# The second FFN product of a two-layer DiT step by seven block products for eight

## What the kernel must compute

```python
x = x + g1 * o
h = modulate(rmsnorm(x, p['norm_ffn_g']), sh2, sc2)
gt, up = jnp.split(h @ p['ffn_w_in'], 2, axis=-1)
return x + g2 * ((jax.nn.silu(gt) * up) @ p['ffn_w_out'])
```

## Time and profile before

| what | value |
|---|---|
| three runs | 1826.86, 1824.64, 1828.18 us |
| median | 1826.86 us |
| profiled execution, span | 1825.5 us (the page gives no other time for it) |
| granted TensorE clock, mean | 0.996 of full speed |
| PE busy | 1741.5 us, 95% |
| DVE, ACT, POOL busy | 58%, 44%, 20% |

### The profile page before, as it was taken

The page is one execution under the profiler, slowest core; times in us unless marked ns, Lnnn a source line. Parts: engine busy times, 40 slices in busy tenths (PEclk is TensorE's granted clock), DMA queues, the critical chain, the costliest instruction groups (busy, mean ns, idle before and its releaser), DMA issues. The chain is left out here.

```text
span 1825.5 us, 46192 instructions
## 1 busy us (share of the span) xinstructions
PE 1741.5 (95%) x19693; PEld 1629.2 (89%) x19693; DVE 1064.4 (58%) x2330; ACT 803.0 (44%) x1729; POOL 370.7 (20%) x306
## 2 busy tenths in 40 slices
PE   7999988889999999999999999898999999999997
PEld 5999776779899999999989987777898999999997
DVE  4545777663494673838453566676519647365663
ACT  3343655542453351535443356464326525344352
POOL 3254010212202003020324431002231120201112
PEclk9999999999999999999999999999999999999999
DMA  9654401004513313141327360010122132323211
GB/s 338 211 131 145 120 5 49 6 4 135 168 59 89 85 60 103 58 115 53 99 83 202 97 193 21 17 36 7 29 66 56 63 108 64 105 61 90 84 56 58
DMA packets 215973, 161.11 MB, mean 88 GB/s; under 512 B 21968, under 2 KB 213146, under 8 KB 215770
## 3 DMA queue, kind: packets, MB, share of 16 engines
q1 hardware_dynamic: 213818, 156.13, 29.0%
q0 software_dynamic: 1952, 2.03, 0.4%
HBM read 154.99 MB, written 3.15 MB: 87 GB/s over the span
## 5 line engine op out<-in xcount | busy, mean ns | idle before, releaser
L2683 DVE SCALAR_TENSOR_TENSOR x<-PS,mod,x 128x320 f32<-128x320 f32 (+2 forms) x240 | 90.8, 434 | 289.3 <-PE PS L1082 289.3
L1118 PE MATMUL PS<-T_hi,wsplit 128*128 128x320 f32 x768 | 170.0, 309 | 0.0
L822 POOL TENSOR_TENSOR SfR<-ring,SfR 128x768 fp32r<-128x768 f32 (+1 forms) x24 | 41.1, 1712 | 582.3 <-ACT SfR L1792 582.3
L1081 PE MATMUL PS<-in_hi,win 128*128 128x320 f32 x480 | 149.9, 320 | 0.7 <-POOL win L822 0.7
L1082 PE MATMUL PS<-in_hi,win 128*128 128x320 f32 x480 | 144.6, 309 | 0.0
L1081 PE MATMUL PS<-hid_hi,wsplit 128*128 128x320 f32 x440 | 133.0, 310 | 0.0
L1082 PE MATMUL PS<-hid_hi,wsplit 128*128 128x320 f32 x440 | 132.5, 309 | 0.0
L1118 PEld LDWEIGHTS PS<-T_hi,wsplit 128*128 128x128 f32 x768 | 128.4, 188 | 0.0
L1118 PE MATMUL PS<-h_hi,wsplit 128*128 128x320 f32 x576 | 127.6, 309 | 0.0
L1118 PE MATMUL PS<-T_lo,wsplit 128*128 128x320 f32 x384 | 118.7, 309 | 0.0
L2110 ACT ACTIVATE wsplit<-Sf 128x512 fp32r<-128x512 f32 x96 | 59.8, 629 | 130.0 <-DVE Sf L2733 72.3
(11 more groups left out here) (540 smaller groups left out, 5407.2 us busy)
## 6 DMA issues: line engine op xcount, KB each, us to landing
ring<-in_w_ada SPq DMA_DIRECT2D x47, 1024.0 KB, 6.7
ring<-in_ffn_w_in SPq DMA_DIRECT2D x88, 512.0 KB, 5.2
ring<-in_ffn_w_out SPq DMA_DIRECT2D x16, 768.0 KB, 4.3
ring<-in_ffn_w_out SPq DMA_DIRECT2D x16, 640.0 KB, 4.0
ring<-in_w_in SPq DMA_DIRECT2D x7, 1024.0 KB, 9.5
ring<-in_w_in SPq DMA_DIRECT2D x10, 512.0 KB, 6.0
ring<-in_w_in SPq DMA_DIRECT2D x16, 256.0 KB, 6.0
ring<-in_w_out SPq DMA_DIRECT2D x16, 256.0 KB, 5.8
```

The lines of the kernel that those rows point to most:

```text
L822: nc.gpsimd.tensor_tensor(lo, raw_w, hi, SUB).then_inc(wl_ready(), 1)
L1081: mm(lat[:, 0:TH], w, v[:, 0:TH], start=(n == 0), stop=(n == total - 1))
L1118: last = mm(bank[:, 0:TH], (w_lo if p == 1 else w_hi)[:, k, :], (v_lo if p == 2 else v_hi)[:, k, :], start=(q in (A11, A12, S1_) and k == ...
L2683: last = V.scalar_tensor_tensor(x[:, m, a:b], bank[:, at:at + b - a], mod[:, gate_at + m, s:s + 1], x[:, m, a:b], MUL, ADD)
```

## The change

The second product of every part is also made by seven block products for eight. Two hidden tiles (a pair: even and odd) and two output tiles (a group mm: 256 columns of the weight) with the left and right 320 tokens make the 2 x 2 blocks. `PARTS` becomes (0,6), (6,12), (12,18), (18,22), so that all parts have whole pairs. For each part there are 4 groups x 7 = 28 products, each over the pairs of the part with 3 passes: 9 matmuls of 320 columns with 6 tiles, 6 with 4. Their order (`second_order`) runs groups 0 and 1 side by side, then 2 and 3:

```diff
-PARTS = ((0, 6), (6, 12), (12, 17), (17, 22))
+PARTS = ((0, 6), (6, 12), (12, 18), (18, 22))
...
+    ahead = [(0, S1_), (0, S3_), (1, S1_), (1, S3_), (0, S2_), (1, S2_)]
+    after = {1: [(0, S4_), (1, S4_)]}
+    for m in (2, 3):
+        at = AT2[part]
+        for n, q in ((at[(m, A11)] - 8, S1_), (at[(m, A11)] - 8, S3_), (at[(m, A11)] - 4, S2_), (at[(m, A12)] - 4, S4_)):
+            after.setdefault(n, []).append((m, q))
...
+LAST_HOOKS = {14: 0, 18: 1, 20: 2, 22: 3, 25: 4}
...
+                def second_low(part, n):
+                    mm_, q = ORDER2[part][n]
+                    hi, lo = second_slot(part, n)
+                    e.wait_ge(f2_hi.sem, f2_upto(f2_hi, l, part, n + 1))
+                    nc.gpsimd.tensor_tensor(lo, second_blocks(l, part, mm_)[q], hi, SUB).then_inc(f2_lo(), 1)
+                def hidden_low(pair, j, q):
+                    hi, lo = block_of(q, j)
+                    e.wait_ge(t2_high.sem, t2_high.upto(l, 4 * pair + T2_AT[q]))
+                    e.wait_ge(t2_sum.sem, t2_sum.upto(l, 4 * pair + max(SUM2_NEEDED[q], {S1_: 3, S2_: 4}.get(q, 0))))
+                    nc.gpsimd.tensor_tensor(lo, block_full(q, j), hi, SUB).then_inc(t2_low(), 1)
+                for part in range(len(PARTS)):
+                    pairs = pairs_of(part)
+                    for j, pair in enumerate(pairs[:-1]):
+                        for q in (S1_, S2_, S3_, A22):
+                            hidden_low(pair, j, q)
+                    j, pair = len(pairs) - 1, pairs[-1]
+                    for n in range(N2):
+                        if n == 5:
+                            hidden_low(pair, j, S1_)
+                            hidden_low(pair, j, S2_)
+                        if n == 6:
+                            hidden_low(pair, j, S3_)
+                            hidden_low(pair, j, A22)
+                        second_low(part, n)
+                        if part == LAST and n in (20, 23):
+                            add_squares(l + 1, 0, {20: 1, 23: 3}[n])
+                add_squares(l + 1, 0, 5)
...
+                def second_product(part, n):
...
+                    e.wait_ge(f2_lo.sem, f2_upto(f2_lo, l, part, n + 1))
+                    if q in (A11, A12):
+                        last_of_bank = A22 if q == A11 else S4_
+                        if mm_ >= 2:
+                            e.wait_ge(f2_read.sem, f2_upto(f2_read, l, part, at[(mm_ - 2, last_of_bank)] + 1))
...
+                    else:
+                        read = {S2_: A11, S3_: S2_, A22: S3_, S1_: A12, S4_: S1_}[q]
+                        e.wait_ge(f2_read.sem, f2_upto(f2_read, l, part, at[(mm_, read)] + 1))
...
+                def second_sum(part, mm_, q):
...
+                    elif q == S2_:
+                        e.wait_ge(f2_sum.sem, f2_sum.upto(l, 16 * part + at[(mm_, S1_)] + 1))
+                        e.wait_ge(f2_lo.sem, f2_upto(f2_lo, l, part, AT2[part][(mm_, A11)] + 1))
+                        out, first, second, op = w[S2_], w[S1_], w[A11], SUB
...
+                    e.wait_ge(right_ready.sem, right_ready.upto(l, si + 1))
+                    hidden_sum(end_pair, end_j, S3_)
+                    left_low(si, tile)
+                    right_low(si, tile)
+                    hidden_sum(end_pair, end_j, S2_)
+                    hidden_sum(end_pair, end_j, A22)
+                    for n in range(N2):
+                        second_read(part, n)
+                        for m, q in sums_after.get(n, ()):
+                            second_sum(part, m, q)
+                        if part < LAST and n == 23:
+                            block_low(FAST[part + 1], 0)
+                            block_low(FAST[part + 1], 1)
```

More of the change, by code:

```diff
@@ L98, in split_units @@
         u += [(("gate", i), ("f1", i), 0, KT), (("up", i), ("f1", i), 1, KT)]
-    for part, (a, b) in enumerate(PARTS):
-        u += [(("f2", m, part), ("f2", 4 * part + m // 2), m % 2, b - a) for m in range(KT)]
     return u
@@ L131, in item_order @@
         o += [("gate", i), ("up", i)]
-    for part in range(len(PARTS)):
-        o += [("f2", m, part) for m in range(KT)]
     return o
@@ L2183, in _ @@
-                    if not final:
-                        for n in range(5):
+                    for n in range(6, N2):
+                        second_high(part, n)
+                        if not final and n == 23:
+                            block_high(FAST[part + 1], 0)
+                            block_high(FAST[part + 1], 1)
+                        if final and n in SQUARE_AFTER:
+                            k = SQUARE_AFTER[n]
+                            e.wait_ge(f2_read.sem, f2_upto(f2_read, l, part, TILE_DONE[k]))
+                            norm_square(l + 1, 0, k)
@@ new lines, in right_low, with hidden_sum @@
+                def right_low(si, tile):
+                    j = tile // 2
+                    if tile % 2 == 1:
+                        V.tensor_tensor(b22_lo[j], f_right(tile), b22_hi[j], SUB).then_inc(hid_split(), 1)
+                def hidden_sum(pair, j, q):
+                    out, first, second, made = {
+                        S1_: (f_left(2 * j), f_right(2 * j), f_left(2 * j), 0),
+                        S3_: (f_right(2 * j), f_right(2 * j + 1), f_right(2 * j), 1),
+                        S2_: (f_right(2 * j + 1), f_right(2 * j + 1), f_left(2 * j), 2),
+                        A22: (f_left(2 * j + 1), f_left(2 * j + 1), f_right(2 * j + 1), 3)}[q]
+                    if made >= 2:
+                        e.wait_ge(t2_sum.sem, t2_sum.upto(l, 4 * pair + made))
+                    V.tensor_tensor(out, first, second, SUB).then_inc(t2_sum(), 1)
@@ new lines, in second_read @@
+                def second_read(part, n):
+                    mm_, q = ORDER2[part][n]
+                    at = AT2[part]
+                    bank = ps[2 + mm_ % 2] if q in (A12, S1_, S4_) else ps[mm_ % 2]
+                    e.wait_ge(f2_done.sem, f2_upto(f2_done, l, part, n + 1))
+                    before = {A12: A11, S3_: S1_, S4_: S2_}.get(q)
+                    if before is not None:
+                        e.wait_ge(f2_read.sem, f2_upto(f2_read, l, part, at[(mm_, before)] + 1))
+                    elif l > 0 or part > 0:
+                        e.wait_ge(f2_read.sem, f2_upto(f2_read, l, part, 0))
+                    m, left = {A11: (0, True), A12: (0, True), S2_: (0, False), S1_: (1, False), S3_: (1, False),
+                               S4_: (0, False), A22: (1, True)}[q]
+                    m += 2 * mm_
+                    for a, b in ((0, TH),) if left else ((TH, NL), (NL, T)):
+                        s = 1 if a == NL else 0
+                        at_ = a if left else a - TH
+                        last = V.scalar_tensor_tensor(x[:, m, a:b], bank[:, at_:at_ + b - a], mod[:, 40 + m, s:s + 1],
+                                                      x[:, m, a:b], MUL, ADD)
+                    last.then_inc(f2_read(), 1)
@@ L2789, in _ @@
                         if si > fast_pairs(part)[0]:
-                            pair_low(si - 1, tile - 1)
+                            left_low(si - 1, tile - 1)
+                            right_low(si - 1, tile - 1)
+                        if done_pair is not None:
+                            hidden_sum(done_pair, done_j, S1_)
+                            hidden_sum(done_pair, done_j, S3_)
+                        if ends:
+                            e.wait_ge(right_ready.sem, right_ready.upto(l, si))
+                            hidden_sum(end_pair, end_j, S1_)
+                            for m, q in sums_ahead[:4]:
+                                second_sum(part, m, q)
                         low_ahead(si, A12)
                         low_ahead(si, S2_)
+                        if done_pair is not None:
+                            hidden_sum(done_pair, done_j, S2_)
                         low_ahead(si, S1_)
@@ L2795, in _ @@
                         product_sum(si, S3_, G5[:, :], own_x, ADD)
+                        if done_pair is not None:
+                            hidden_sum(done_pair, done_j, A22)
                         low_ahead(si, S3_)
-                        product_sum(si, S4_, E2, ps[5], ADD)
+                        product_sum(si, S4_, right, ps[5], ADD)
                         low_ahead(si, S4_)
+                        if ends:
+                            for m, q in sums_ahead[4:]:
+                                second_sum(part, m, q)
                         e.wait_ge(g_sig.sem, g_sig.upto(l, 2 * si + 1))
```

324 lines of the change are left out of this document (242 added, 82 removed).

## The result

The changed kernel takes 1878.67 us (median of four runs, 1873.13 to 1887.37); the kernel before took 1827.52 beside it. The ratio is 1.0281 [1.0248, 1.0314]: slower by 2.8%, about 51 us, where 42 had been forecast.

A forecast was written before the change was run, and what follows sets the result against it. TensorE, busy 95% of the span, was taken as the bound. Per layer 40.6 us lost against 19.4 gained made 21.2 slower, 42.4 in two, so 1869 us; main case 1857 to 1880 (chance 0.50), range 1832 to 1892.

The forecast's parts named there:

- Turns: Both products: a VectorE instruction with SBUF operands and a GpSimd subtraction run one after the other, about 1.38 us a turn.
- A full part: Second product with six tiles, second and third parts: waits ahead of four products lose 7.9 us together.
- product 2: Start of the second product: waits for the last odd tile's low part behind VectorE and GpSimd turns, 1.7 us lost.
- product 6: Second product: GpSimd's row of hidden and second-weight low parts, with VectorE's sums between, comes late, 1.6 us lost.
- Product 13: Second product, group 2: waits for reading 11, behind three VectorE sums each waiting for GpSimd; 3.4 us lost, the largest term.
- Product 27: End of the second product: the next part's weight sums and low parts stand ahead of reading 25, 1.2 us lost.
- The first part: Second product of a layer's first part: second-weight work starts after the last silu and multiplication, so 9.8 us lost.
- First product: Tiles finishing a pair: four more VectorE sums and GpSimd's low parts, 0.9 us lost in each of seven, 6.3 a layer.
- The last part and the end: Four-tile part: 7.1 us lost plus 0.5 for squares; afterwards 0.8 in layer 0, some 1.4 in layer 1.
- Side by side: Rival: VectorE and GpSimd do not block each other; 16.7 us lost against 19.4 a layer, 1821 us, chance 0.16.
- Half turns: Rival: GpSimd not behind at product 9, so product 13 loses 0.8 us for 3.4; 1848 us, chance 0.20.
- First product bound by VectorE: Rival: GpSimd's four low parts of a pair are not absorbed, 2.2 us a tile for 0.9; 1887 us, chance 0.10.

The follow-up runs named there:

- small kernel: Separate kernel, VectorE and GpSimd alone, then together: alone an instruction every 0.47 and 0.95 us, together with all operands in SBUF every 1.27 us each.
- sums from PSUM: Kernel after, one operand of VectorE's hidden-block and second-weight sums read from PSUM, in all parts but the last: 1847.63 us, ratio 1.0095.
- experiment 8: Kernel after, VectorE's four sums for each pair finished in the first product done on 16 of 320 columns: 1873.37 us, ratio 1.0229.
- experiment 2: Kernel before, only the parts cut as in the change (6, 6, 6, 4 tiles), second product still by eight: 1830.09 us, ratio 1.0006.
- spread sums: Kernel after, a finished pair's sums in the first product set apart, only S1 ahead of the reading of S3: 1876.7 us, ratio 1.0271.
- two moves: Kernel after, second-weight sums of groups 2 and 3 behind later readings and the next part's weight sums further apart: 1840.35 us, ratio 1.0086.

## Why the prediction was right, and where its sizes were off

*What is saved, and what bounds.* 264 matmuls fewer, at the old rate where nothing waits (36.97 us for 252, against the forecast's 37.0). Right.

*Turns.* Right, and shown twice: in the small kernel and by the sums from PSUM. The Trainium skill (SBUF — State Buffer, Who interferes with whom) calls the shared ports an exclusive lock; by that rule the trace agrees (30.4 us for 22.9), with 0.15 us of each turn overlapping after all.

*A full part.* Forecast 7.9 us lost, measured 44.64 - 36.97 = 7.7 where the clock is full. An idle time that the trace lists costs 0.26 us more than its length, from matmul start to matmul start (in part 2 of layer 0 the five listed waits are 6.4 us, the loss 7.7). With that added:
- product 2: forecast 1.7, measured 0.8. The term was mis-sized: a product waits pair by pair, so only its last three matmuls, those of the last pair, wait for `right_low`, and the six ahead of them are 0.9 us more cover than I gave it.
- product 5: forecast nothing, measured 0.7, the same GpSimd row that makes 6 late.
- product 6: 1.6, measured 1.6. Product 13: 3.4, measured 3.3. Product 27: 1.2, measured 1.3.

*The first part.* Forecast 9.8, measured 48.05 - 36.97 = 11.1 in layer 0, of which about 1.5 are low clock.

*First product.* 6.3 a layer forecast, 4.8 measured (0.9 against 0.78 a pair, and in the first part 0.9 for two pairs). The mechanism was as forecast: GpSimd's first `hidden_low` has 0.8 us in the sum, and the trace shows it holding up a weight sum by 0.71 us ahead of each wait, beside sums of 0.40 from start to start. Which of the two would have to go is not shown (experiment 8).

*Layer 0 up to its last part, first products included.* By the forecast's terms 248.3 (first products of before) + 6.3 + 3 x 37.0 + 9.8 + 2 x 7.9 = 391.2 us; measured 390.5 (375.1 in the kernel before with the same cut, experiment 2; the 368.1 us of the kernel before hold one tile less of the second product).

*The last part and the end.* In layer 1 the forecast's 7.6 us and the end's 1.4 are 9.0, and 9.0 were measured (52.8 from the last part's start to the end, 54.3 before, with 72 matmuls or 10.6 us fewer). In layer 0 8.4 were forecast and 13.8 measured. Waits of that stretch (L1022 is `add_squares`):

```profile
PE PS L1289 <- DVE x L3037: 2.7, 1, 2.7
PE PS L1092 <- POOL mix L1022: 1.9, 2, 1.7
PE PS L1289 <- POOL wsplit L1040: 1.6, 2, 1.4
PE PS L1289 <- DVE bl_lora L2988: 1.3, 1, 1.3
```

The squares on GpSimd cost 1.7 us for the 0.5 that I had, and the granted clock was 0.76 from 932.0 to 939.0 and 0.77 from 945.0 to 952.3, which is another 3.4 us.

*The clock: the term that was missing.* The forecast priced a wait at its length. Behind product 13 it costs up to 2.8 us more: parts two and three of layer 1 take 47.40 and 47.41 us, the second part of layer 0 44.64, with the same waits to a few hundredths. In the kernel after the low clock once came earlier, behind the 1.36 us of product 6 in the third part of layer 0:

```profile
818.60:829.50 10.90, 8.62 (x56) 7.83 (x54) 10.55 (x18) 5.83 (x14) 9.48 (x10) 1.00 0.01 2
829.50:836.00 6.50, 6.46 (x33) 6.46 (x34) 3.69 (x8) 1.57 (x3) 6.50 (x7) 0.74 0.00 0
836.00:842.00 6.00, 4.60 (x32) 4.34 (x30) 5.35 (x10) 2.10 (x4) 6.00 (x6) 1.00 1.07 279
```

There it cost nothing: TensorE came to product 13 that much later, waited 1.5 us for 3.0, and the part took 44.66. Over the kernel: 1.5 in part one of layer 0, 3.4 in its last, 2.8 in each of layer 1's first three, together 13 of the 17.6 us by which the span (60.0 more) exceeds the forecast (42.4). Another 4.5 lie between the two FFNs, in work that the change doesn't touch (472.9 us for 468.4, from the first matmul behind the FFN of layer 0 to the first product of layer 1). They too go with the clock, which is at its lower level twice in that stretch and nowhere in the same stretch of the kernel before:

```profile
1177.70:1181.10 3.40, 3.40 (x104) 3.40 (x97) 1.74 (x8) 0.00 (x0) 0.00 (x0) 0.50 0.00 0
1269.90:1276.70 6.80, 6.27 (x58) 5.54 (x59) 2.06 (x9) 2.08 (x5) 0.00 (x0) 0.50 0.01 2
```

Half of the busy time in them is 4.8 us; why it fell there is open. What is left nearly cancels: the first FFN starts 2.2 us later than before, the last part of layer 0 loses 2.0 more than forecast apart from its clock, the first products 3.0 less. That the median (1878.67) still lies within the 1857 to 1880 of the main case, 1.3 us from its edge, is in part luck: the profiled run lies outside. The runs that were not profiled are 9 to 14 us shorter than the profiled one, and their clock was 0.987 to 0.990 on average for 0.983.

*Rivals.* Side by side: out. Half turns: out, `second_low(13)` was waited for 1.22 us and the three sums took 1.28 each. First product bound by VectorE: half true. VectorE, with GpSimd's turns in its queue, is what limits those tiles, as the spread sums show, but by 0.78 us a pair and without the lateness that goes on.

## What to carry to other kernels

Before engines are given new work side by side, look for operands: a VectorE instruction that combines two tensors in SBUF and a subtraction of GpSimd went in turns in every trace here, so their times add, and a queue of one that was sized alone is late. Ask of each row of small sums which reading stands behind it; moving six of a part's sixteen behind later readings took over half of the net loss away (35 of 60 us by the spans) with the same work. When an experiment makes an instruction shorter, look in its trace whether the turns around it have moved too. And price a wait of TensorE of about 3 us above its length: here 0 to 2.8 us more.

## What was not expected of the hardware

Behind waits of the same length, 3.0 to 3.2 us with full work around them, the granted clock fell in some parts and not in others, and the part took 0, 1.5 or 2.8 us more for it; in three traces (after, sums spread, two moves) it fell once behind a wait of 1.35 us that had two of 0.5 ahead of it, while the single ones of 1.7 in the kernel before left it at 1.00. The Trainium skill (TensorE: Matmul & The Clock Gate, HAM oscillation — how this bites in real kernels) tells that gaps between a kernel's matmuls can bring the lower clock back, each time anew; the traces agree for four of the six waits of 3.1 us put into the kernel before and for both of 3.4 and 3.5. Why one wait is followed by the low clock and its twin isn't, no run here tells.
